# Expert stage of a decoder trunk: regrouped columns and a packed stationary for the second token tile

## The reference

```python
def swiglu(x, w_gu, w_down):
    g, u = jnp.split(x @ w_gu, 2, axis=-1)
    return (jax.nn.silu(g) * u) @ w_down

def moe_swiglu(x, w_router, w_gu, w_down):
    logits = jnp.einsum('bsd,de->bse', x, w_router).astype(jnp.float32)
    top_val, top_idx = lax.top_k(logits, TOP_K)          # 2 of 8
    gates = jax.nn.softmax(top_val, axis=-1)
    ...
    for e in range(N_EXPERTS):
        out = out + gate_full[..., e:e + 1] * swiglu(x, w_gu[e], w_down[e])
```

## Time and profile before

| | |
|---|---|
| Median of 3 runs | 1339.68 us (1334.26 to 1347.05) |
| The profiled execution | 1336.62 us, its span 1334.9 us |
| TensorE busy | 1269.2 us (95%) |
| VectorE busy | 649.6 us (49%) |
| ScalarE busy | 531.8 us (40%) |
| Expert loop | from 961.2 to 1263.9 us of the span |
| Granted clock, mean | 0.983 |

### The profile page before, as it was taken

One profiled execution on the slowest core, in us unless ns is written; L12 is line 12 of the kernel. 1 busy time (PEld: TensorE's weight loads), 2 busy tenths in 40 slices (PEclk: granted clock), 3 DMA queues, 4 the chain that ended last, 5 costly groups with the idle time before them and its releaser, 6 DMA issues.

```text
span 1334.9 us, 17356 instructions
## 1 busy us (share of the span) xinstructions
PE 1269.2 (95%) x6465; PEld 1078.6 (81%) x6466; DVE 649.6 (49%) x848; ACT 531.8 (40%) x708; POOL 42.6 (3%) x64
## 2 busy tenths in 40 slices
PE   7999999999999999999999999999789899999868
PEld 6889998578888878886778789985679798988757
DVE  5334444633333332323653355445675465568874
ACT  3225442442323331123432233324654454467742
POOL 0000000000000000000000000000110110111100
PEclk9999999999999999999999999999899899999979
DMA  7331112333333342321326733222696695779951
GB/s 191 95 95 51 52 58 63 95 103 101 95 94 94 94 124 87 94 65 53 98 79 102 83 68 49 63 81 63 213 337 187 222 296 176 236 217 362 324 224 57
DMA packets 198951, 174.92 MB, mean 131 GB/s; under 512 B 7344, under 2 KB 179440, under 8 KB 198896
## 3 DMA queue, kind: packets, MB, share of 16 engines
q1 hardware_dynamic: 195008, 160.01, 41.4%
q0 software_dynamic: 3312, 12.06, 2.5%
q10 hardware_dynamic: 576, 2.10, 0.4%
HBM read 164.19 MB, written 9.96 MB: 130 GB/s over the span
## 4 chain that ended last, share of the span: by engine, by line
PE 85%; DVE 5%; ACT 3%; issue 3%; DMA 3%; ACTq 0%; SPq 0%; DVEq 0%; POOLq 0%
PE bank L722 27%; PE bank L724 26%; PE bank L723 26%; DMA ring<-moe_w_down 2%; PE bank L816 1%; DVE w_lo L1701 1%; ACT w_hi L1579 1%; PE bank L1086 1%; DVE x_exact L1819 1%; PE bank L1039 1%; PE bank L1134 1%; PE bank L905 0%; PE bank L909 0%; DVE x_lo L1827 0%; ACTq L1553 0%
## 5 line engine op out<-in xcount | busy, mean ns | idle before, releaser
L1701 DVE TENSOR_TENSOR w_lo<-raw,w_hi 128x1024 fp32r<-128x1024 f32 (+5 forms) x212 | 287.2, 1362 | 186.6 <-ACT w_hi L1253 134.3
L722 PE MATMUL bank<-x_hi,w_hi 128*128 128x512 f32 x672 | 265.1, 394 | 11.6 <-DVE w_lo L1701 4.7
L724 PE MATMUL bank<-x_hi,w_lo 128*128 128x512 f32 x672 | 263.2, 392 | 0.0
L723 PE MATMUL bank<-x_lo,w_hi 128*128 128x512 f32 x672 | 262.9, 391 | 0.0
L1253 ACT CAST w_hi<-raw 128x1024 fp32r<-128x1024 f32 (+3 forms) x133 | 143.2, 1077 | 217.4 <-PE bank L724 217.4
L722 PE MATMUL bank<-w_hi,x_hi 128*128 128x256 f32 (+2 forms) x608 | 190.4, 313 | 13.1 <-issue 9.0
L723 PE MATMUL bank<-w_lo,x_hi 128*128 128x256 f32 (+2 forms) x608 | 188.0, 309 | 0.0
L724 PE MATMUL bank<-w_hi,x_lo 128*128 128x256 f32 (+2 forms) x608 | 188.0, 309 | 0.0
L722 PEld LDWEIGHTS bank<-x_hi,w_hi 128*128 128x128 f32 x672 | 127.1, 189 | 44.6 <-DVE w_lo L1701 7.6
L724 PEld LDWEIGHTS bank<-x_hi,w_lo 128*128 128x128 f32 x672 | 126.9, 189 | 26.6
L723 PEld LDWEIGHTS bank<-x_lo,w_hi 128*128 128x128 f32 x672 | 127.1, 189 | 25.5
(11 more groups left out here) (318 smaller groups left out, 1722.4 us busy)
## 6 DMA issues: line engine op xcount, KB each, us to landing
raw<-moe_w_gu SPq DMA_DIRECT2D x32, 768.0 KB, 5.7
raw<-ffn_w_gu SPq DMA_DIRECT2D x44, 512.0 KB, 3.8
raw<-a_w_qkv SPq DMA_DIRECT2D x24, 512.0 KB, 3.7
...
```

Source lines behind the costliest of these rows:

```text
L722: pe.matmul(o, s_hi, m_hi, start=start, stop=False, skip_group_check=True)
L723: pe.matmul(o, s_hi, m_lo, start=False, stop=False, skip_group_check=True)
L724: return pe.matmul(o, s_lo, m_hi, start=False, stop=stop, skip_group_check=True)
L1701: return dve.tensor_tensor(dst, a, b, ALU.subtract)
```

## The change

The columns of a gate or up product are no longer taken as 384 and 320. Chunks 0 to 2 are 512 columns of gate over all eight k-tiles (three, three and two of them), chunks 3 to 5 the same of up. Chunks 6 and 7 hold the other 192 columns of gate and of up side by side, 384 in one bank; their two parts are loaded by two DMAs. The down product is cut as before. A plain tile then has 9, 9, 6, 9, 9, 6 products of 512 columns, 12 and 12 of 384, and 36 of 512.

The second tile of an expert with two tiles is packed: its stationary has the high parts of up to 64 tokens in columns 0 to 63 and the low parts of the same tokens in columns 64 to 127. Two products, with `w_hi` and with `w_lo`, give in rows 0 to 63 the products of the high parts and in rows 64 to 127 those of the low parts. ScalarE copies rows 64 to 127 down to rows 0 to 63, and VectorE adds. For the output the upper rows go to `y_part`, and GpSimd adds them before the store, for which it reads the number of tiles twice. The number of tiles becomes three (the four-tile body) from 193 tokens on, no longer from 257. The hidden tile is now 512 and 192 columns wide, in four and two tiles of 128; the first is transposed after chunk 6.

```diff
-FC = (3 * P, FE - 3 * P)
+FW = 512
+FR = FE - FW
...
+def chunk_size(c):
+
+    return (1536, 1536, 1024, 1536, 1536, 1024)[c] if c < 6 else 1536
+
+
+def rest_bank(t, n):
+
+    return 2 + t if n <= 2 else t
+
+
 def hidden_bank(half, t, n):
 
-    return 2 + t if half == 0 and n <= 2 else 4 + t
+    return 6 + t if half == 0 and n <= 2 else 4 + t
+
+
+HALF = P // 2
+
+
+def packed(t, n):
+
+    return n == 2 and t == 1
+
+
+def hidden_tiles(half):
+
+    return slice(0, FW // P) if half == 0 else slice(FW // P, KE)
...
-                for c in range(8):
-
-                    half, up, kh = c // 4, c // 2 % 2, c % 2
-                    col = up * FE + half * FC[0]
+                for c in range(6):
+
+                    k0, nk, col = c % 3 * 3, (3, 3, 2)[c % 3], c // 3 * FE
                     if c == 3:
                         sp_eng.wait_ge(xg_loaded, 16 * TT)
-                    src = moe_w_gu[0][bass.ds(e, 1), kh * 4 * P:(kh + 1) * 4 * P, col:col + FC[half]]
+                    src = moe_w_gu[0][bass.ds(e, 1), k0 * P:(k0 + nk) * P, col:col + FW]
                     raw_free(e, c)
-                    sp_eng.dma_start(flat(c % SLOTS, 4, FC[half]), src.rearrange("e (k p) n -> p (e k) n", p=P)
-                                     ).then_inc(raw_loaded[c % SLOTS], 16)
+                    sp_eng.dma_start(flat(c, nk, FW), src.rearrange("e (k p) n -> p (e k) n", p=P)
+                                     ).then_inc(raw_loaded[c], 16)
+                for c in (6, 7):
+
+                    s, raw_at = c % SLOTS, flat(c % SLOTS, 4, 2 * FR)
+                    src = moe_w_gu[0][bass.ds(e, 1), (c - 6) * 4 * P:(c - 5) * 4 * P, :]
+                    raw_free(e, c)
+                    sp_eng.dma_start(raw_at[:, :, 0:FR], src[:, :, FW:FE].rearrange("e (k p) n -> p (e k) n", p=P)
+                                     ).then_inc(raw_loaded[s], 16)
+                    sp_eng.dma_start(raw_at[:, :, FR:2 * FR], src[:, :, FE + FW:2 * FE].rearrange("e (k p) n -> p (e k) n", p=P)
+                                     ).then_inc(rest_loaded[s], 16)
...
+                def add_halves(n):
+                    if n == 2:
+                        y = y_tok[1][0:HALF, :].rearrange("p (k n) -> p k n", n=2 * P)
+                        pool.tensor_tensor(y, y, y_rest, ALU.add).then_inc(y_added, 1)
+                    else:
+                        pool.nop().then_inc(y_added, 1)
+
                 def store(n):
                     for t in range(n):
-                        pool.indirect_dma_start(y_dram, bass.IndirectOffsetOnAxis(ap=store_i[:, t:t + 1], axis=0),
-                                                y_tok[t][:, :], None).then_inc(y_stored, 16 * share(t, n))
+                        r = HALF if packed(t, n) else P
+                        pool.indirect_dma_start(y_dram, bass.IndirectOffsetOnAxis(ap=store_i[0:r, t:t + 1], axis=0),
+                                                y_tok[t][0:r, :], None).then_inc(y_stored, 16 * share(t, n))
+
+                def count():
+                    return pool.value_load(tiles_i[0:1, bass.ds(e, 1)], min_val=1, max_val=TT)
                 pool.tensor_copy(store_i[:, :], place_i[:, bass.ds(TT * e, TT)]).then_inc(indexed, 1)
                 pool.wait_ge(indexed, indexed_to)
 
                 pool.wait_ge(banks_out, 8 * e + 16)
-                by_tiles(pool, pool.value_load(tiles_i[0:1, bass.ds(e, 1)], min_val=1, max_val=TT), store)
+                by_tiles(pool, count(), add_halves)
+                pool.wait_ge(y_added, e + 1)
+                pool.nop().then_inc(y_summed, 1)
+                by_tiles(pool, count(), store)
...
+            def packed_mm(o, s_both, m_hi, m_lo, start, stop):
+
+                pe.matmul(o, s_both, m_hi, start=start, stop=False, skip_group_check=True)
+                return pe.matmul(o, s_both, m_lo, start=False, stop=stop, skip_group_check=True)
+
+            def x_columns(o, t, n, kk, c, w):
+
+                m_hi, m_lo = w_hi[c % DEEP][:, w], w_lo[c % DEEP][:, w]
+                if packed(t, n):
+                    return packed_mm(o, x_hi[:, kk, P:2 * P], m_hi, m_lo, kk == 0, kk == KD - 1)
+                return mm3(o, x_hi[:, kk, t * P:(t + 1) * P], x_lo[:, kk, t * P:(t + 1) * P], m_hi, m_lo,
+                           kk == 0, kk == KD - 1)
...
-                        if c == 2:
+                        if c == 3:
 
                             pe.wait_ge(banks_out, 8 * e + 8)
-                        if c == 4:
+                        if c == 6 and n > 2:
 
                             pe.wait_ge(silu_ready, 8 * e + TT)
-                        if c == 6 and n > 2:
-
-                            pe.wait_ge(het_ready, 8 * e + TT)
                         for t in range(n):
-                            mm = first_half(t, c, e)
+                            mm = wide_columns(t, c, n) if c < 6 else rest_columns(t, c, n)
...
-                        if c == (5 if n <= 2 else 4):
+                        if c == 6:
...
-                        if c in (1, 5):
-                            half = c // 4
-                            act.wait_ge(chunk_done, 4 * q0 + 12 * e + c + 1)
+                        if c == 2:
+                            act.wait_ge(chunk_done, 4 * q0 + 12 * e + 3)
+                            if n == 2:
+                                act.copy(he[0:HALF, 2, 0:FW], bank[1][HALF:P, :]).then_inc(packed_moved, 1)
+                            else:
+                                act.nop().then_inc(packed_moved, 3)
                             for t in range(n):
-                                act.activation(he[:, t, half * FC[0]:half * FC[0] + FC[half]],
-                                               bank[t][:, 0:FC[half]], ACT.Silu).then_inc(silu_ready, share(t, n))
-                        if c in (5 if n <= 2 else 4, 8):
+                                if packed(t, n):
+                                    act.wait_ge(packed_sum, 3 * e + 1)
+                                    act.activation(he[0:HALF, 1, 0:FW], he[0:HALF, 1, 0:FW], ACT.Silu).then_inc(silu_ready, share(t, n))
+                                else:
+                                    act.activation(he[:, t, 0:FW], bank[t][:, :], ACT.Silu).then_inc(silu_ready, share(t, n))
+                        if c == 5 and n == 2:
+                            act.wait_ge(chunk_done, 4 * q0 + 12 * e + 6)
+                            act.copy(he[0:HALF, 3, 0:FW], bank[5][HALF:P, :]).then_inc(packed_moved, 1)
+                        if c == 7:
+                            act.wait_ge(chunk_done, 4 * q0 + 12 * e + 8)
+                            if n == 2:
+                                act.copy(he[0:HALF, 2, 0:2 * FR], bank[3][HALF:P, 0:2 * FR]).then_inc(packed_moved, 1)
+                            for t in range(n):
+                                if packed(t, n):
+                                    act.wait_ge(packed_sum, 3 * e + 3)
+                                    act.activation(he[0:HALF, 1, FW:FE], he[0:HALF, 2, 0:FR], ACT.Silu).then_inc(silu_ready, share(t, n))
+                                else:
+                                    act.activation(he[:, t, FW:FE], bank[rest_bank(t, n)][:, 0:FR], ACT.Silu
+                                                   ).then_inc(silu_ready, share(t, n))
...
+                            if packed(t, n):
+                                act.copy(y_tok[1][0:HALF, f], b[0:HALF, :])
+                                act.copy(y_rest[:, c % 2 * 2:c % 2 * 2 + 2, :], b[HALF:P, :].rearrange("p (k n) -> p k n", n=2 * P)
+                                         ).then_inc(banks_out, share(t, n))
+                            else:
+                                act.copy(y_tok[t][:, f], b[:, :]).then_inc(banks_out, share(t, n))
...
-            dve.scalar_tensor_tensor(out=tiles_f[1][:, 0:NE], in0=counts, scalar=2.0 * P, in1=tiles_f[0][:, 0:NE],
+            dve.scalar_tensor_tensor(out=tiles_f[1][:, 0:NE], in0=counts, scalar=1.5 * P, in1=tiles_f[0][:, 0:NE],
                                      op0=ALU.is_gt, op1=ALU.add).then_inc(slot_step, 1)
...
+            dve.memset(he[HALF:P, 1, 0:FE], 0.0)
...
-                        if c in (3, 7):
-                            half = c // 4
-                            dve.wait_ge(chunk_done, 4 * q0 + 12 * e + c + 1)
+                        if c == 2:
+                            if n == 2:
+                                dve.wait_ge(packed_moved, 3 * e + 1)
+                                dve.tensor_tensor(he[0:HALF, 1, 0:FW], he[0:HALF, 2, 0:FW], bank[1][0:HALF, :], ALU.add
+                                                  ).then_inc(packed_sum, 1)
+                            else:
+                                dve.nop().then_inc(packed_sum, 3)
+                        if c == 5:
+                            dve.wait_ge(chunk_done, 4 * q0 + 12 * e + 6)
                             for t in range(n):
```

(27 more changed lines are left out.)

89 lines of the change are left out of this document (55 added, 34 removed).

## The result

The changed kernel took 1317.2 us (median of 6 runs, 1314.1 to 1323.0) where the kernel before took 1339.8 beside it: a ratio of 0.984, 95% interval 0.981 to 0.987. Two later sets of six runs gave 1319.3 and 1317.3 (medians). The forecast was 1314, with a range of 1303 to 1325. The profiled execution took 1314.1 us, its span is 22.5 us shorter, and the sum had said 23.4 less.

What follows compares the result with a forecast made beforehand. It took TensorE to bound two-tile experts, TensorE and weight transfers together one-tile experts. Terms -24.8 + 0 + 1.4 = -23.4 gave 1313.2 from the profiled 1336.6, or 1316.3 by the median; it said 1314, range 1303 to 1325.

Steps and rivals of the forecast that it cites:

- Parts (1) and (2): Regrouped columns save 0.25 us a tile; with two packed products for three, each two-tile expert is 8.28 us shorter.
- Part (3): Packed tile's extra ScalarE copies and VectorE additions in two-tile experts: counted at nothing, covered by one chunk of products.
- bare hand-overs: Copy, add, silu, multiply chains end late, up to 3.2 us in each two-tile expert: 1323; chance 0.12.
- Part (4): One-tile experts: new 0.5 us wait at first transposes, cancelled at the second; nothing for five, within -3 and +5 us.
- Part (5): Gate and up weight transfers in rows of 2048 and 768 bytes, same bytes, two more issues an expert: nothing.
- Part (6): GpSimd's second read of the tile count before its store, behind the last expert: +1.4 us, bounds 0.5 and 2.
- Gap gone: One of TensorE's two 4.5 us waits, at the first two-tile expert and the next, disappears: 1306; chance 0.15.
- Narrow rows: Packets of 768 bytes cost what 1 KB did, adding 1.5 us to each of five one-tile experts: 1321; chance 0.08.
- no packing: The second tile of a two-tile expert still has three products: 1337; chance 0.02.
- More tiles: One expert with 193 to 256 tokens runs the four-tile body, 96 us instead of 50: 1368; chance 0.03.

Runs made afterwards that it cites:

- the columns alone: The changed kernel with its regrouped columns but no packing, the second tile keeping three products: 1340.9 us, 1.0007 of the kernel before.
- wide rows: The changed kernel with chunks 6 and 7 each loaded by one DMA of 1536-byte rows instead of two of 768: 1317.2 us, ratio 0.983.

## Why the prediction was right, and which term was mis-sized

**Parts (1) and (2)**, the regrouping and the packed tile, held: -0.25 us a tile (measured 0.5 and 0.6 for two tiles), and 8.28 us an expert (8.4 and 8.3 in experts 3 and 4; 7.2 in expert 1, in a window with a clock of 0.94 where it had been 0.97). That a packed product costs what a plain one does was taken without a row; here it is, TensorE in expert 4 across the seam of the tiles:

```profile
1113.61 0.39 PE L776 MATMUL bank<-w_lo,x_hi 128*128 128x512 f32 x1
1113.83 0.39 PE L777 MATMUL bank<-w_hi,x_lo 128*128 128x512 f32 x1
1114.06 0.39 PE L1163 MATMUL bank<-w_hi,x_hi 128*128 128x512 f32 x1
1114.29 0.39 PE L1164 MATMUL bank<-w_lo,x_hi 128*128 128x512 f32 x1
1114.51 0.39 PE L1163 MATMUL bank<-w_hi,x_hi 128*128 128x512 f32 x1
```

Steps of 0.22 to 0.23 us on both sides, as in the earlier trace rows. The Trainium skill's 0.216 ("TensorE: Matmul & The Clock Gate", "Back-to-back issue gap") would by the prediction's estimate have made both parts together 7.5 us an expert; the measurement says 8.4 and 8.3, so here the row decides.

**Part (3)**, copies and additions at nothing, held inside the two-tile experts, with less to spare than it said. VectorE and ScalarE in expert 4, from the full bank of chunk 5 to the transposes:

```profile
1130.35 0.59 ACT L1677 COPY he<-bank 64x512 f32<-64x512 f32 x1 [0.79 <-PE bank L1164]
...
1131.28 0.68 DVE L2298 TENSOR_TENSOR he<-he,bank 128x512 f32<-128x512 f32 x1
1131.87 0.67 DVE L2293 TENSOR_TENSOR he<-he,bank 64x512 f32<-64x512 f32 x1
1132.74 0.68 DVE L2298 TENSOR_TENSOR he<-he 64x512 f32<-64x512 f32 x1 [0.19 <-DVE he L2293]
...
1133.64 1.03 PE L1205 MATMUL bank<-ident,he 128*128 128x128 f32 x8
```

The chain from the start of the copy to the end of the last multiply takes 3.1 us, where 2.7 was worked out, and it ends 0.2 us before TensorE asks; TensorE doesn't wait there, nor anywhere in the two-tile experts for the hidden tile. That answers the rival of bare hand-overs.

What the part missed lies in the next expert. It counts ScalarE's copies and VectorE's additions, but has no term for GpSimd's own addition of the two halves of the output (L737). Expert 5 of the changed kernel:

```profile
1156.81 2.40 POOL L737 TENSOR_TENSOR y_tok<-y_tok,y_part 64x1024 f32<-64x1024 f32 x1 [6.27 <-issue]
1157.69 3.14 DVE L1797 TENSOR_TENSOR w_lo<-raw,w_hi 128x1536 fp32r<-128x1536 f32 x1 [3.19 <-ACT w_hi L1650]
...
1160.96 0.49 PE L775 MATMUL bank<-w_hi,x_hi 128*128 128x512 f32 x1 [1.53 <-DVE w_lo L1797]
```

The same split with the columns alone, where GpSimd adds nothing:

```profile
1182.93 1.76 DVE L1797 TENSOR_TENSOR w_lo<-raw,w_hi 128x1536 fp32r<-128x1536 f32 x1 [4.46 <-ACT w_hi L1650]
```

ScalarE's cast of this chunk begins 2.3 us after the expert's start in both, and the split 3.9 us after it. But while GpSimd adds, the split takes 3.14 us in place of 1.76, and TensorE waits 1.5 us for it. In each of the eleven traces with packing three splits run beside such an addition, and they take 2.8 to 3.1 us; no other split of the loop takes over 1.9, and none does in the two traces without packing. No run moved the addition to another time, so the cause rests on this coincidence. Without the packing expert 5 is 1.0 us shorter (27.4 for 28.4). It costs once: expert 4 has such a split too, but two tiles of products cover it, and expert 2 begins with a gap.

**Part (4)** is the term that was mis-sized: nothing for the five one-tile experts, within -3 and +5 us. The step that failed is the walk "cast 1.49, split 1.76, multiply 0.65": it begins with the cast of chunk 8 at the end of chunk 4, as if its load were always there. Where it was, the wait was 0.50 us to the hundredth. Where it was not, in experts 6 and 7 and, in two traces of three, in expert 0, it was 1.1 to 2.7 us, and behind the longest of these waits TensorE ran on at half clock. The changed kernel in expert 6, and in expert 0, from the end of the wait:

```profile
1198.17:1200.20 2.03, 2.03 (x8) 2.03 (x9) 1.75 (x2) 0.82 (x2) 0.00 (x0) 0.50 1.04 237
...
976.24:979.50 3.26, 3.26 (x12) 3.26 (x13) 2.52 (x3) 2.01 (x3) 0.00 (x0) 0.50 1.04 315
```

A granted clock of 0.50 is 1.2 GHz; the products of 384 columns come every 0.32 us in place of 0.174, and expert 6 pays the wait (2.26) and some 1.3 us on top: 27.08 with a wait of 0.5, 30.18 here. The text had the clue: it said that transfers and TensorE bind the short experts together, and then used that only to argue that a gain would be lost, not that a new dependence on a load would cost. Experts 5 to 7 grew by 4.6 us on average over three traces; expert 5's 0.7 is the matter of part (3), and 3.9 are those of experts 6 and 7, inside the bounds of +5. By the text's own words, the forecast fails where short experts grow by over 1 us each, and two of these three did. The cancelling that it counted on, of the new wait against the old one before the second transposes, did happen in expert 5, whose old wait of 1.5 us went; in experts 6 and 7 the old ones were 0.5 and 0.65.

**Part (5)**, the rows, held: wide rows changed nothing clear of the spread (1317.2 us, for 1319.3 and 1317.2 of the changed kernel). **Part (6)**, the second read: +1.4 was said, +1.0 measured, within the bounds.

**The rivals.** Gap gone: both gaps are still there in every trace, 3.3 to 3.6 us and 2.8 to 3.2 in the changed kernel. The Trainium skill ("Runtime: NRT & Kernel Launch", "Instruction fetch mechanics") says that a branch to a block that isn't in TensorE's memory of 2048 instructions forces a fetch. By that rule the prediction let the one on returning go, as the loop is now shorter than that; it stayed in all three traces, so they do not bear this out. Why each got about 1 us shorter was not tested. Narrow rows are excluded by the wide ones, and "no packing" by the products of expert 4 and by the columns alone. "More tiles" did not occur, as no expert of the changed kernel exceeds 48 us; what the four-tile body would cost was not tried.

The forecast of 1314 was therefore right in its mechanism and some 3 us low against the median of 18 runs, 1317.3; by the median of before the sum itself had said 1316.3. The size of part (4) is the larger part of what it missed, and in the profiled execution the 5 us from the gaps and expert 2, which no term had, hid it.
